# Two transformer blocks in float32 on one core: how the last expert pairs are combined and written

## The chip, the core and the metric

One core of a Trainium2 chip runs the whole program. The metric is the device time of one execution in microseconds, as the median of several runs. The engines are named as in the profile: PE (TensorE, matrix products), DVE (VectorE), ACT (ScalarE), POOL (GpSimd), SP (SyncE, which here only issues transfers). Everything is float32, so that a product of 128 x 128 with 128 x 512 is two MATMUL records on PE.

## The reference, cut to what matters

There are two blocks over 512 tokens of width 1024. The first has an SSD mixer, attention and a feed-forward part; the second has attention, an mLSTM branch and, at its end, a mixture of 32 experts. Only this end matters here:

```python
h = rmsnorm_2(x, norm2_g)
# each token: one group of 8 experts, in it the two best, weights top_w
y_row = (silu(xb @ w_gate[e]) * (xb @ w_up[e])) @ w_down[e]      # 1024 -> 512 -> 1024
y = zeros((T, D)).at[row_tok].add(y_row * row_w)                 # two rows per token
out = x + y
```

## The kernel before, in words

The 512 tokens are four tiles of 128 (`xtok[:, t, :]`, in SBUF, tokens on partitions). Each expert has room for 64 rows, and the experts are taken in 16 pairs, so that a pair fills 128 rows. Experts 0 and 1 are pair 0, and so on to pair 15, the last one.

For a pair, PE (function `pair` in the tensor block) multiplies the rows of the pair, which it picked out of `xtok` with a 0/1 matrix in `pick_rows`, with the gate slabs of its two experts, then with the up slabs (L1436, `both_k`: two products side by side in the two halves of the array), picks the rows of the next pair (L1445), transposes the inner rows `hE` (L1452, `turn_inner`) and multiplies with the down slabs (L1436 again) into banks 6 and 7. ACT applies Silu (L2849), copies the transposed inner rows (L2854) and empties banks 6 and 7 into `ysb` (L2858, L2861). For pairs 0 to 14 ACT then writes `ysb` to the scratch tensor `ys_d` in HBM (L2864). DVE multiplies gate and up (L2437), scales the picked rows (L2429) and makes the 0/1 matrices `pick` for the pair after the next (`picks`, L2400 and L2404). With `weighted=True` it makes another one, `wpick` (L2409, L2413), in which a token's router weight stands instead of the 1.

A slab is a [128 x 4096] tile, 2 MB. There are nine places for slabs (`ws`), used in turn (`turn9`). SP issues all slab loads in one order in its queue (`next_slab`, L607): two gate slabs, two up slabs, two down slabs of each pair, each as soon as the product that used its place has ended (`g_full`, `uu_full`, `yy_full` count these products).

The last pair does not go through `ys_d`. PE transposes `wpick` (L1469), ACT copies it to `wpT` (L2852), and PE multiplies it with `ysb` into the eight banks (L1531, eight products of 128 x 128 with 128 x 512, in the order `LAST`). All other rows are fetched by POOL: after the last write to `ys_d` (`y_st`) it gathers, for each tile and each of the token's two experts, 128 rows of 4 KB (L2938, eight gathers of 512 KB into the places `ws[7]` and `ws[8]`; rows that belong to the last pair read zeros, which POOL wrote at the start, L2923). DVE adds each gather times its weight to `xtok` (L2497), and after all of these the eight banks (L2503). `comb` counts those sums, and SP writes tile after tile to `out` (L617). The order on each engine is the order of the code.

## Time and profile before

| | before |
|---|---|
| median of 3 runs | 1761.68 us (1761.37 to 1761.73) |
| profiled execution | 1762.02 us |
| its span, first to last instruction | 1760.2 us |
| PE busy | 1701.0 us, 97% |
| DVE busy | 775.6 us, 44% |
| ACT busy | 329.4 us, 19% |
| POOL busy | 18.7 us, 1% |
| HBM read, written | 319.66 MB, 18.37 MB |
| mean granted clock of PE | 0.987 |

PE is called busy nearly throughout, but a busy share says little of what bounds a stage, since records of products overlap and their ends are modelled. For the last stage one reads what the DMA engines do in a stretch, then the chain of waits from the end backwards, then each engine by time.

### The profile page before, as it was taken

The numbers are of one execution on the slowest core, as the hardware profiler recorded it, in microseconds if no ns is written. First come the engines' busy times: TensorE is split into PE (matmuls) and PEld (weight loads), VectorE is DVE, ScalarE is ACT, GpSimd is POOL, SyncE is SP. The second block draws the span as 40 slices with busy tenths as digits, with TensorE's granted clock in tenths as the row PEclk, the third lists the DMA queues.
The fourth block names the chain that finished last, engine by engine and source line by source line (L and its number), as shares of the span: only waits on it lengthen the run. The fifth ranks groups of instructions, "written<-read, shape, count | busy, mean of one in ns | idle before, by whom it ended". The sixth has DMA issues, their size and how long they took to land.

```text
span 1760.2 us, 19911 instructions
## 1 busy us (share of the span) xinstructions
PE 1701.0 (97%) x7884; PEld 1054.2 (60%) x7884; DVE 775.6 (44%) x1711; ACT 329.4 (19%) x691; POOL 18.7 (1%) x39
## 2 busy tenths in 40 slices
PE   8999999999999999999999999999799999999997
PEld 5445544488888888878444454447645455544452
DVE  4322448677777772354796233325522121211123
ACT  1121224231111100120234234201200000000000
POOL 0001000000000000000000000000000000000001
PEclk9999999999999999999999999999899999999999
DMA  9874120022122213141211110313489999999997
GB/s 404 330 281 161 60 95 2 1 81 96 57 86 95 81 67 131 48 158 54 96 48 49 48 48 1 143 48 143 189 349 428 429 429 429 429 429 429 429 428 316
DMA packets 30248, 335.62 MB, mean 191 GB/s; under 512 B 3208, under 2 KB 5784, under 8 KB 10592
## 3 DMA queue, kind: packets, MB, share of 16 engines
q1 hardware_dynamic: 22464, 310.56, 43.4%
q10 hardware_dynamic: 5168, 14.91, 2.2%
q0 software_dynamic: 2544, 9.18, 1.5%
q8 instruction: 47, 0.77, 0.2%
q14 instruction: 25, 0.20, 0.0%
HBM read 319.66 MB, written 18.37 MB: 192 GB/s over the span
## 4 chain that ended last, share of the span: by engine, by line
PE 85%; DMA 6%; DVE 6%; ACT 2%; issue 1%; POOL 0%; SPq 0%; DVEq 0%; ACTq 0%; POOLq 0%
PE bank L1436 15%; PE bank L1039 15%; PE bank L1087 8%; PE bank L1445 6%; PE bank L1222 5%; PE bank L646 4%; PE bank L850 3%; PE bank L1230 3%; PE bank L1131 3%; PE bank L1394 3%; PE bank L1180 3%; DMA arena<-in_w_expert_up 2%; DMA pool<-in_w_expert_up 2%; PE bank L995 2%; PE bank L628 2%; PE bank L840 2%
## 5 line engine op out<-in xcount | busy, mean ns | idle before, releaser
L1436 PE MATMUL bank<-pool,arena 128*64 128x512 f32 x1216 | 337.8, 598 | 8.5 <-DMA pool<-in_w_expert_up 3.9
L1039 PE MATMUL bank<-pool 128*128 128x256 f32 x1232 | 267.6, 381 | 0.8 <-ACT pool L2510 0.8
L1039 PEld LDWEIGHTS bank<-pool 128*128 128x128 f32 x1232 | 235.5, 191 | 32.8 <-issue 1.0
L1436 PEld LDWEIGHTS bank<-pool,arena 128*64 128x64 f32 x1216 | 108.0, 138 | 175.9 <-issue 167.6
L2437 DVE TENSOR_TENSOR arena<-arena,bank 128x512 f32<-128x512 f32 x16 | 11.0, 688 | 281.5 <-PE bank L1436 281.5
L1445 PE MATMUL bank<-arena 128*128 128x128 f32 x1024 | 123.7, 281 | 8.5 <-DVE arena L2404 8.5
L1445 PEld LDWEIGHTS bank<-arena 128*128 128x128 f32 x1024 | 119.4, 196 | 20.8 <-issue 12.2
L1222 PE MATMUL bank<-pool 128*128 128x512 f32 x256 | 114.5, 595 | 1.9 <-DVE arena L2203 1.9
L1222 PEld LDWEIGHTS bank<-pool 128*128 128x128 f32 x256 | 47.4, 190 | 58.4 <-issue 54.9
L1436 PE MATMUL bank<-xT,arena 128*64 128x512 f32 x160 | 72.3, 606 | 3.8 <-DMA pool<-in_w_expert_up 3.8
L1436 PE MATMUL bank<-arena 128*64 128x512 f32 x160 | 70.3, 593 | 0.0
L2429 DVE TENSOR_TENSOR arena<-bank,cols 128x512 f32<-128x512 f32 x32 | 22.1, 692 | 103.6 <-PE bank L1445 103.6
L646 PE MATMUL bank<-pool 128*128 128x512 f32 x144 | 63.8, 597 | 0.0
L1180 PE MATMUL bank<-pool 128*128 128x512 f32 x128 | 60.7, 610 | 1.5 <-ACT arena L2510 1.5
L2694 ACT ACTIVATE arena<-arena,cols 128x512 f32<-128x512 f32 x44 | 29.4, 714 | 173.1 <-DVE arena L1940 173.1
L1087 PE MATMUL bank<-arena,pool 128*128 128x256 f32 x264 | 58.5, 379 | 0.0
L850 PE MATMUL bank<-pool 128*128 128x512 f32 x128 | 56.7, 594 | 0.0
L1087 PEld LDWEIGHTS bank<-arena,pool 128*128 128x128 f32 x264 | 50.3, 190 | 6.7
L2510 ACT ACT_TABLE_LOAD x39 | 50.0, 1283 | 19.5 <-DVE small L1649 16.9
L1847 DVE TENSOR_TENSOR pool<-pool 128x1024 f32<-128x1024 f32 x44 | 52.8, 1220 | 0.3
L2510 ACT ACTIVATE arena<-bank 128x512 f32<-128x512 f32 (+4 forms) x62 | 29.2, 490 | 119.4 <-PE bank L646 51.3
L2510 ACT ACTIVATE pool<-bank 128x512 f32<-128x512 f32 (+3 forms) x73 | 31.4, 462 | 96.0 <-PE bank L850 45.2
(418 smaller groups left out, 2180.8 us busy)
## 6 DMA issues: line engine op xcount, KB each, us to landing
pool<-in_w_expert_gate SPq DMA_DIRECT2D x27, 2048.0 KB, 25.8
pool<-in_w_expert_down SPq DMA_DIRECT2D x27, 2048.0 KB, 28.0
pool<-in_w_expert_up SPq DMA_DIRECT2D x22, 2048.0 KB, 23.2
pool<-in_w_in SPq DMA_DIRECT2D x15, 2048.0 KB, 8.2
pool<-in_w_ada SPq DMA_DIRECT2D x12, 2048.0 KB, 19.2
pool<-in_w_up SPq DMA_DIRECT2D x11, 2048.0 KB, 8.0
arena<-in_w_expert_gate SPq DMA_DIRECT2D x5, 2048.0 KB, 29.8
xT<-in_w_expert_up SPq DMA_DIRECT2D x5, 2048.0 KB, 24.8
```

The source lines that it names most:

```text
L646: ins = pe.matmul(bank[home[g]][:, :], w[:, k, c0:c0 + P], src[:, k, :], start=(k == 0), stop=(k == KD - 1))
L850: ins = pe.matmul(bank[home[g0 + c]][:, :], w[:, k, c * P:(c + 1) * P], hT[:, k, :], start=(k == 0), stop=(k == KD - 1))
L1039: ins = pe.matmul(up_quarter(u, p), lhs[:, k, :], rhs[:, k, :], start=(k == 0), stop=(k == 3))
L1087: ins = pe.matmul(dst, lhs[:, i, :], rhs[:, i, :], start=(i == 0 and p in (0, 1, 4)), stop=(i == HP - 1), skip_group_check=p not in (0, 1, 4))
L1131: ins = pe.matmul(bank[qa_bank(u, p)][:, 0:256], lhs[:, k, :], rhs[:, k, :], start=(k == 0 and p in (0, 1, 4)), stop=(k == 3), skip_group_ ...
L1180: ins = pe.matmul(bank[home[g0 + t]][:, :], hT[:, k, t * P:(t + 1) * P], w[:, k, :], start=(k == 0), stop=(k == KD - 1))
L1222: ins = pe.matmul(bank[home[g]][:, :], w[:, k, o:o + P], hT[:, k, :], start=(k == 0), stop=(k == KD - 1))
L1230: ins = pe.matmul(bank[home[g]][:, :], w[:, k, m * P:(m + 1) * P], src[:, k, :], start=(k == 0), stop=(k == 3))
L1394: ins = pe.matmul(dst, lhs[:, k, :], rhs[:, k, :], start=(k == 0 and p in (0, 1, 4)), stop=(k == 3), skip_group_check=p not in (0, 1, 4))
L1436: ins = pe.matmul(dst[b * CAP:(b + 1) * CAP, :], lhs(b, k), rhs(b, k), start=(k == 0), stop=(k == n_k - 1))
L1445: ins = pe.matmul(bank[x][:, f * P:f * P + n], xtok[:, t, c], pick[:, t, 0:n], start=(t == 0), stop=(t == NT - 1))
L2510: ins = nc.scalar.activation(dst, src, f, **kw)
```

## The change

The rows of pair 14 are no longer written to `ys_d` and gathered. DVE makes a weighted matrix for it too (`wpick2`), PE transposes it in pair 14 (`weights_turned`), and multiplies it with `ysb` in the last pair's body: two products behind the gate product, three behind the up product, three behind the transposes of the inner rows (`combined`), into banks 0 and 1 in turn; DVE adds each to `xtok` (`summed`). The gathers of tiles 0 and 1 start when pair 13's rows are written and pair 14's up product has ended; they go to `ws[6]`, and DVE adds them before it multiplies gate and up of the last pair. The gathers of tiles 2 and 3 go to `ws[7]` and wait until the last down slabs have landed. The two last down slabs are loaded in halves of their columns (first halves of both, then second halves), the down product of the last pair signals each half, ACT empties each half, `LAST` goes over the four tiles by column halves, and the sums and writes to `out` are by halves too. One more block of zeros is written to `ys_d` at the start. Three semaphores that guarded what other waits guard as well are gone (`alog_exp`, `z_sig`, `ov_sp`).

```diff
-        LAST = ((0, 0), (1, 0), (0, 1), (1, 1), (2, 0), (2, 1), (3, 0), (3, 1))
+        LAST = tuple((t, half) for half in range(2) for t in range(4))
@@ SP
-                for r in range(15):
+                for r in range(13):
                     next_slab(4, r)
-                for t in range(NT):
-                    sp.wait_ge(S["comb"], LAST.index((t, 1)) + 1)
-                    sp.dma_start(out[t * P:(t + 1) * P, :], xtok[:, t, :]).then_inc(S["out_st"], 16)
+                sp.wait_ge(S["g_full"], 15)
+                sp.wait_ge(S["uu_full"], 15)
+                for half in range(2):
+                    c = slice(half * 512, (half + 1) * 512)
+                    for b in range(2):
+                        at = turn9[(6 * 15 + 4 + b) % 9]
+                        sp.dma_start(slot(at, 4, D)[:, :, c], down_of(30 + b).rearrange("p (k n) -> p k n", n=D)[:, :, c])\
+                          .then_inc(S["ed_half"] if half else landed[at], 16)
+                for n, (t, half) in enumerate(LAST):
+                    c = slice(half * 512, (half + 1) * 512)
+                    sp.wait_ge(S["comb"], 9 + n)
+                    sp.dma_start(out[t * P:(t + 1) * P, c], xtok[:, t, c]).then_inc(S["out_st"], 16)
@@ PE
+                def weights_turned(n):
+                    pe.wait_ge(S["pick_rdy"], E // 2 + 2 * n)
+                    if n:
+                        pe.wait_ge(S["wp_ev"], 1)
+                    for t in range(NT):
+                        ins = pe.transpose(bank[5][:, t * P:(t + 1) * P], (wpick2, wpick)[n][:, t, :], ident[:, :])
+                    ins.then_inc(S["wp_full"], 1)
+                def combined(n0, n1):
+                    pe.wait_ge(S["wp_ev"], 1)
+                    pe.wait_ge(S["yy_ev"], E // 2 - 1)
+                    for n in range(n0, n1):
+                        t, half = LAST[n]
+                        if n >= 2:
+                            pe.wait_ge(S["comb"], n - 1)
+                        pe.matmul(bank[n % 2][:, :], wpT2[:, t, :], ysb[:, half * 512:(half + 1) * 512], start=True, stop=True)\
+                          .then_inc(S["add_full"], 1)
@@ PE, pair(p, at, first, last, late)
+                        if last and half == 0:
+                            combined(0, 2)
...
+                        weights_turned(1)
+                        combined(2, 5)
                     pe.wait_ge(S["he_rdy"], p + 1)
                     turn_inner()
...
+                    else:
+                        combined(5, 8)
+                    if late:
+                        weights_turned(0)
...
+                        if last and half:
+                            pe.wait_ge(S["ed_half"], 32)
@@ DVE
+                pair(E // 2 - 4, False, False)
+                picks(E // 2 - 2, weighted=wpick2)
                 pair(E // 2 - 3, False, False)
-                picks(E // 2 - 1, weighted=True)
+                picks(E // 2 - 1, weighted=wpick, more=1)
                 pair(E // 2 - 2, False, False)
-                pair(E // 2 - 1, False, True)
+                gathered(0)
+                summed(0, 2, lambda n: n % 2)
+                gathered(1)
+                pair(E // 2 - 1, False, True)
+                summed(2, 8, lambda n: n % 2)
+                summed(8, 10, lambda n: n % 8)
+                gathered(2)
+                summed(10, 11, lambda n: n % 8)
+                gathered(3)
+                summed(11, 16, lambda n: n % 8)
@@ POOL
-            for r0 in range((E - 2) * CAP, ROWS, P):
+            for r0 in range(ZR, ROWS, P):
...
-                po.wait_ge(S["y_st"], 16 * (E // 2 - 1))
+                po.wait_ge(S["y_st"], 16 * (E // 2 - 2))
+                po.wait_ge(S["uu_full"], E // 2 - 1)
                 for t in range(NT):
+                    if t == 2:
+                        po.wait_ge(S["yy_full"], E // 2 - 1)
+                        po.wait_ge(S["ed_half"], 32)
```

`gathered(t)` waits for its gathers (one semaphore for tiles 0 and 1, another for 2 and 3) and makes the two weighted additions of the tile; `summed(n0, n1, ...)` adds the banks of those combining products, each to half a tile.

## Rows read from the trace of the kernel before

**Rows 1.** Windows by stage: engines' busy time, granted clock, DMA share, GB/s.

```profile
core 0: us, PE busy (x) PEld busy (x) DVE busy (x) ACT busy (x) POOL busy (x), PEclk, DMA share, GB/s
1400.00:1450.00 50.00, 50.00 (x298) 26.54 (x296) 9.80 (x26) 3.16 (x6) 0.00 (x0) 1.00 1.01 429
1720.00:1730.00 10.00, 7.82 (x38) 2.79 (x36) 0.00 (x0) 0.60 (x1) 0.65 (x1) 1.00 1.01 428
1740.00:1750.00 10.00, 9.22 (x32) 3.68 (x29) 8.99 (x7) 1.08 (x2) 0.00 (x0) 0.96 0.46 184
```

**Rows 2.** Chain of waits, last 60 us: start us, us, what.

```profile
1705.45 0.44 PE bank L1452 x4
...
1717.93 10.57 DMA ys_d<-arena
...
1733.21 7.53 DMA xT<-ys_d,smi
...
1740.76 1.29 DVE arena L2497
...
1751.33 1.88 DVE arena L2503 x3
```

**Rows 3.** Timeline of PE: start us, us, line, what, idle time before it.

```profile
1664.37 0.61 PE L1436 MATMUL bank<-xT,arena 128*64 128x512 f32 x1 [2.00 <-DMA pool<-in_w_expert_up]
...
1721.46 1.89 PE L1436 MATMUL bank<-pool,arena 128*64 128x512 f32 x8
1725.53 7.09 PE L1436 MATMUL bank<-pool,arena 128*64 128x512 f32 x32 [2.18 <-DMA pool<-in_w_expert_up]
...
1736.19 8.78 PE L1436 MATMUL bank<-pool,arena 128*64 128x512 f32 x32 [2.07 <-DMA pool<-in_w_expert_down]
1745.75 7.10 PE L1531 MATMUL bank<-arena 128*128 128x512 f32 x16 [0.78 <-ACT arena L2858]
```

**Rows 4.** Window over the zero fill, and POOL's wait behind it.

```profile
150.00:185.00 35.00, 35.00 (x143) 19.28 (x142) 13.10 (x30) 7.22 (x12) 7.36 (x10) 1.00 0.55 173
...
POOL arena L2926 <- PE bank L1087: 591.0, 1, 591.0
```

**Rows 5.** Timeline of DVE, pairs 13 to 15 and the end.

```profile
1673.25 0.69 DVE L2437 TENSOR_TENSOR arena<-arena,bank 128x512 f32<-128x512 f32 x1 [21.17 <-PE bank L1436]
...
1684.48 2.14 DVE L2409 TENSOR_SCALAR arena<-arena,small 128x128 f32<-128x128 f32 x8
1686.66 0.69 DVE L2413 TENSOR_TENSOR arena<-arena 128x512 f32<-128x512 f32 x1
1701.79 0.69 DVE L2437 TENSOR_TENSOR arena<-arena,bank 128x512 f32<-128x512 f32 x1 [14.44 <-PE bank L1436]
...
1750.01 1.28 DVE L2497 SCALAR_TENSOR_TENSOR arena<-xT,small,arena 128x1024 f32<-128x1024 f32 x1
1751.33 4.87 DVE L2503 TENSOR_TENSOR arena<-arena,bank 128x512 f32<-128x512 f32 x8
```

**Rows 6.** DMA queues in 1721:1728, 1729:1735, 1753:1760.2: packets, MB, share.

```profile
q1 hardware_dynamic: 164, 2.42, 80.9%
q10 hardware_dynamic: 143, 0.52, 18.3%
...
q1 hardware_dynamic: 150, 2.13, 83.3%
q0 software_dynamic: 90, 0.35, 14.5%
...
GB/s 0 0 0 0 0 0 478 410 364 387 410 432 387 387 455 432 387 364 410 364 364 478 364 455 455 387 410 364 364 478 364 455 432 387 228 0 0 0 0 0
q1 hardware_dynamic: 576, 2.10, 73.0%
```

**Rows 7.** Timeline: issues of ACT and SP.

```profile
1689.40 0.34 ACTq L2864 DMA_DIRECT2D ys_d<-arena  x1
...
1695.23 6.82 SPq L607 DMA_DIRECT2D pool<-in_w_expert_down  x2
...
1701.73 0.33 SPq L607 DMA_DIRECT2D pool<-in_w_expert_down  x1
...
1753.23 3.32 SPq L617 DMA_DIRECT2D out<-arena  x4
```

**Rows 8.** Windows of 3 us behind three of PE's waits; columns as in rows 1.

```profile
1666.00:1669.00 3.00, 3.00 (x8) 0.91 (x6) 0.00 (x0) 0.00 (x0) 0.00 (x0) 0.50 0.99 421
...
1726.00:1729.00 3.00, 3.00 (x17) 1.20 (x15) 0.00 (x0) 0.00 (x0) 0.00 (x0) 1.00 1.04 445
...
1738.00:1741.00 3.00, 3.00 (x10) 0.98 (x8) 0.24 (x1) 0.00 (x0) 0.93 (x1) 0.53 1.03 410
```

More of the change, by code:

```diff
@@ L396, in two_blocks @@
                             ("i15", (OVB + 1,)),
-                            ("la", (NT, 36)), ("g7", (7,)), ("cm", (E, 7)), ("pre", (NT, E)), ("bs", (E,)), ("row", (P,)), ("slo", (2, NT))):
+                            ("la", (NT, 36)), ("g7", (7,)), ("cm", (E, 7)), ("pre", (NT, E)), ("bs", (E,)), ("row", (P,)), ("slo", (2, NT)))
+        for name, shape in RS:
             R[name] = view(arena, r_at, *shape)
@@ L401, in two_blocks @@
         wt = sm(2, NT)
+        wpick2 = R["be"].rearrange("p a b -> p (a b)").rearrange("p (t s) -> p t s", s=P)
+        at_ = [n for n, _ in RS].index("oh1")
+        wpT2 = view(arena, 13312 + sum(int(np.prod(w)) for _, w in RS[:at_]), NT, P)
         io_i = smi[:, 0:32]
@@ L1453, in turn_inner, with pair @@
                     ins.then_inc(S["ht_full"], 1)
-                def pair(p, at, first=False, last=False):
+                def weights_turned(n):
[14 more added lines that the diff above has]
+                          .then_inc(S["add_full"], 1)
+                def pair(p, at, first=False, last=False, late=False):
                     pe.wait_ge(S["xt_ev"], p * 2 + 2)
@@ L1525, in _ @@
                 for p in range(13, E // 2):
-                    pair(p, [placed(0, 6 * p + c) for c in range(6)], last=(p == E // 2 - 1))
-                pe.wait_ge(S["xt_ev"], E + 1)
+                    pair(p, [placed(0, 6 * p + c) for c in range(6)], last=(p == E // 2 - 1), late=(p == E // 2 - 2))
+                pe.wait_ge(S["wp_ev"], 2)
+                pe.wait_ge(S["comb"], 8)
                 for n, (t, half) in enumerate(LAST):
@@ L2393, in _, with picks @@
                 seq(ve.tensor_copy(slot_i, R["sl"].rearrange("p b t -> p (b t)")))
-                def picks(i, weighted=False):
+                def picks(i, weighted=None, more=0):
                     for t in range(NT):
@@ L2402, in picks @@
                     ins.then_inc(S["pick_part"], 1)
-                    ve.wait_ge(S["pick_part"], i * 2 + 1)
+                    ve.wait_ge(S["pick_part"], i * 2 + (more + 1))
                     ve.tensor_tensor(pick, pick, pickb, ALU.add).then_inc(S["pick_rdy"], 1)
-                    if weighted:
-                        ve.wait_ge(S["pick_rdy"], i + 1)
+                    if weighted is not None:
+                        ve.wait_ge(S["pick_rdy"], i + more + 1)
                         for t in range(NT):
-                            for b, dst_ in enumerate((wpick, pickb)):
+                            for b, dst_ in enumerate((weighted, pickb)):
                                 ins = ve.tensor_scalar(dst_[:, t, :], R["row"], R["sl"][:, b, t:t + 1], wt[:, b, t:t + 1],
@@ L2612, in _ @@
                 ac.wait_ge(S["ld_rows"], 16)
-                act(expa, row("a_log"), ACT.Exp, "alog_exp")
+                act(expa, row("a_log"), ACT.Exp)
                 ac.wait_ge(S["lx_rdy"], 1)
@@ L2785, in _ @@
                 own("act_free")
-                act(omtok, omtok, ACT.Sigmoid, "z_sig")
+                act(omtok, omtok, ACT.Sigmoid)
                 for x in range(2 * MH):
@@ L2844, in _, with pair @@
             if on("end"):
-                def pair(p, first, last):
+                def pair(p, first, last, late=False):
                     ac.wait_ge(S["g_full"], p + 1)
@@ L2850, in pair @@
                     if last:
-                        ac.wait_ge(S["xt_full"], E + 1)
-                        nc.scalar.activation(wpT.rearrange("p t s -> p (t s)"), bank[5][:, :], ACT.Copy).then_inc(S["xt_ev"], 1)
+                        ac.wait_ge(S["wp_full"], 2)
+                        nc.scalar.activation(wpT.rearrange("p t s -> p (t s)"), bank[5][:, :], ACT.Copy).then_inc(S["wp_ev"], 1)
                     ac.wait_ge(S["ht_full"], p + 1)
                     nc.scalar.activation(hET.rearrange("p k r -> p (k r)"), bank[4][:, :], ACT.Copy).then_inc(S["ht_ev"], 1)
+                    if late:
+                        ac.wait_ge(S["wp_full"], 1)
+                        nc.scalar.activation(wpT2.rearrange("p t s -> p (t s)"), bank[5][:, :], ACT.Copy).then_inc(S["wp_ev"], 1)
                     ac.wait_ge(S["yy_full"], p + 1)
-                    if not first:
+                    if last:
+                        ac.wait_ge(S["add_full"], 8)
+                    elif not first:
                         ac.wait_ge(S["y_st"], p * 16)
@@ L2860, in pair @@
                         ins.then_inc(S["yy_ev"], 1)
+                        ac.wait_ge(S["yy_full"], p + 2)
                     nc.scalar.activation(ysb[:, 512:D], bank[7][:, :], ACT.Copy).then_inc(S["yy_ev"], 1)
-                    if not last:
+                    if not last and not late:
                         ac.wait_ge(S["yy_ev"], p + 1)
@@ L2888, in _ @@
                 pair(0, True, False)
-                with ac.Fori(1, E // 2 - 1) as p:
+                with ac.Fori(1, E // 2 - 2) as p:
                     pair(p, False, False)
+                pair(E // 2 - 2, False, False, late=True)
                 pair(E // 2 - 1, False, True)
```

65 lines of the change are left out of this document (33 added, 32 removed).

## The prediction

> **What bounds the kernel now.** I read first the windows by stage: from 1300 us to about 1744 us the DMA engines are full, at 428 to 429 GB/s while PE is "busy" beside them [rows 1]. This is the stream of expert slabs (2.1 MB each, 4.9 us at that rate), six of them for each of 16 pairs of experts. Then the chain of waits, from its end backwards [rows 2]: sums of DVE from the matmul banks (L2503), eight weighted additions of gathered rows (L2497), the wait for the gathers, their issues by POOL, the write of pair 14's rows to `ys_d`, and before that PE. The chain ends in DVE: gathered rows of tile 0 are there at 1740.76, then 8 additions of 1.32 us and 8 sums of 0.61 us, 15.4 us without a hole, then the last writes. Third, PE by time [rows 3]: it waits 2.18 us for the last up slab (starts 1725.53), 2.07 us for the last down slab (starts 1736.19), ends the down product at 1744.97 and the eight combining products at 1752.85, 3.4 us before DVE. So PE has slack behind the last slabs, DVE has none, and the last slabs are early enough. The question is what the change does to these three.
>
> **Removed waits and bookkeeping.** `alog_exp`, `z_sig`, `ov_sp` and the tenth block of zero fill (instead of nine) are all before or outside the last stage. The fill lies at 161 to 178 us, with DMA share 0.55 [rows 4], and POOL, its issuer, then waits 591 us for other work; another 512 KB there is covered. If its cover were gone it would cost 1.3 us. The removed waits stand behind waits on the same or a later event; taken at 0, bound plus or minus 0.1. `picks(14)` now also makes weights: 8 tensor_scalar and one addition, 2.14 + 0.69 us of DVE [rows 5], in a pair in which DVE idles over 20 us: 0.
>
> **The write of pair 14 goes.** 0.52 MB leave the stream [rows 6]; that is 1.2 us of DMA, of which some 0.2 MB (0.5 us) had gone ahead of the last up slab. POOL need not wait for it: its gathers now hang on pair 13's write (issued 1689.40; the next one took 10.57 us to land [rows 2, 7]) and on pair 14's up product, whose end released SP at 1701.73 and DVE at 1701.79 [rows 5, 7].
>
> **Gathers of tiles 0 and 1, early.** Four of the eight go from behind the last slabs to before them. POOL is released at about 1701.8 instead of 1728.5. In the trace a gather's bytes begin to flow some 4.5 us after the release under the full stream: q0 has moved 0.35 MB by 1735 [rows 6]. So 1706.5 here. How fast do they go against the stream? The nearest row is the write to `ys_d`, 0.52 MB in pieces of 4 KB like the gather's: it takes about 6 us and the slabs get 2.42 MB in the 7 us around it [rows 6]. Four gathers take so some 24 us, to about 1730.5. Their 2.1 MB are paid by the slabs, since the engines were full. Ahead of the last up slab pass 1.9 MB, 4.4 us at 429 GB/s; less the 0.5 us of the write that went: the last up slab lands 3.8 us later (bounds: 2.5, if the gathers share worse; 4.4, if all of them pass). **PE starts its up product at 1729.3 instead of 1725.53.** This is the term that decides.
> Here the Trainium skill says another thing: "DMA: Bandwidth & Descriptors", Queues, rings and completion order, has each DMA engine change between queues only after a whole packet of typically 9 to 17 descriptors. A write of 8 pieces per engine would by that be through in little over a microsecond; in this trace it takes 6 us, so the trace does not agree. By the page all four gathers would be ahead of the last up slab, and the sum would be 0.6 us more.
>
> **Down slabs by halves.** Both are issued at 1701.7; before, one was issued at 1695.23 and the other at 1701.73. With at least three slabs still queued nothing runs dry. The pieces are 2 KB instead of 16 KB. The trace shows 4 KB pieces at about 400 GB/s (the writes to `out` [rows 6]), slabs at 429; I take 390, and half of the rate as the other bound. First halves land near 1734, second ones near 1740 (1748 at half rate). PE asks for them at 1744.0 and 1747.5 (below), so this costs 0; at half rate it just touches.
>
> **PE behind the up slab.** Two of the eight combining products for pair 14's rows lie in PE's wait for the slab (0.89 us each, 7.10 us for eight [rows 3]), and so do the transposes of pair 14's weights (0.44 us, like those of L1452 [rows 2]): free. PE ended its gate product at 1723.35; with these 2.2 us it is 1725.6, and the wait is still 3.7 us. Behind a wait of 2.00 us and one of 2.07 us PE's granted clock fell to 1.2 GHz (0.50 and 0.53 of full in slices of 3 us), and the down product took 8.78 instead of 7.04 us; behind one of 2.18 us it stayed at 2.4 GHz [rows 2, 3, 8]. I expect a fall here, and 1.4 us for it (0 to 1.74: part of it may lie in the idle time). Then, one after the other: up product 7.09, transposes of weights 0.44, three products 2.66, transposes of the inner rows 0.44, three products 2.66, down product 7.04 at full clock. Together 20.33 + 1.4 = 21.7, so **PE ends its down product at 1751.0**, against 1744.97.
>
> **DVE beside it.** Before `hE` of the last pair DVE now has, in its order, two tiles of gathered rows and two sums: 2.64 + 1.22 + 2.64 = 6.5 us from the landing of gather 4. Landing near 1731 makes it free at 1737.5, up product done at 1737.8: covered by 0.3 us only. PE's fifth product waits for the third sum, likewise within 0.5 us. Taken at 0, bound +1.7.
>
> **Gathers of tiles 2 and 3** wait for the second halves: 1740 + 4.5 us for the four issues and the start + 3.5 to 5 us of data gives 1748 to 1749. POOL queues nothing behind them. DVE asks for them at 1753.5: covered by over 4 us.
>
> **The end.** Behind 1751.0: two products (1.78) and a sum (0.69) for the sums that DVE does before it takes gathered rows, to 1753.5. Then tile 2 (2.64), one sum (0.61), tile 3 (2.64), five sums (3.05): 8.94, to 1762.4. PE's other products (done 1758.1) are not late. Last write: 0.85 us from issue to first bytes as at 1753.23, 0.65 us for 256 KB, 0.9 from the last bytes to the end, as in the rows [rows 6, 7], with 0.1 of queue: 2.5. **End 1764.9 against 1760.2: +4.7 us.** The profiled execution is 1762.02, 0.34 over the median, so the median becomes 1761.68 + 4.7 = 1766.4 (+0.27%).
> The same page of the Trainium skill, Bandwidth, says to batch DMAs to 1 MiB or more, and gives 2.0 us plus the bytes at 436 GB/s for one. That speaks against writes of 256 KB. Here four writes of 512 KB went back to back, 2.10 MB in about 5.3 us [rows 6], so a fixed part does not add up and I leave it out; by the page, with the last six writes one behind the other, the end would be near 1772.
>
> **Rivals.**
> 1. *The clock stays at 2.4 GHz and the gathers share worse.* 1.4 and 1.3 us less: +2.0, 1763.7. For it: one wait of 2.18 us had no fall. Against: the wait is longer now.
> 2. *The early gathers cost the stream nothing.* If the slabs kept their time and lost only the write, the up product would start at 1725.0, the down product end at 1745.3 (its clock is not cut by a 3.6 us wait), and 13.9 us behind it the span ends at 1759.2: -1.0 us, 1760.7. It decides while the up product starts not later than 1726.0. DMA at 428 GB/s throughout speaks against it. More gain is not to be had: DVE needs 11.4 us behind the down product however early the gathers are.
> 3. *DVE is held by gathers 0 to 3.* If they land after 1731.3, every further microsecond goes to `hE`, the transposes and the down product. Landing at 1734 makes +7.2, 1768.9.
> 4. *The change does not do what it says*: the second gathers or half slabs late by over 5 us, for instance at half rate with a late start; +8 or more.
> 5. *The writes by halves each pay in full.* The six that follow 1757 at 2.4 us each (0.85 + 0.65 + 0.9, from the rows) end at 1771.4, which makes 1772.9. Against: four writes went back to back. The Trainium skill's rule above would make it so.
>
> **How the numbers follow.** About 0.2%, 3.5 us, is what a measurement can tell here. Forecast as worked out 0.50 (1765.2 to 1768.0), rival 1 0.20, rival 2 0.11, rival 3 0.10, rival 4 0.02, rival 5 0.01, none of these 0.06. Slower: 0.50 + 0.10 + 0.02 + 0.01, less 0.03 of the forecast that may fall below 1765.2: 0.60. Same: 0.20 + 0.11 + 0.03 = 0.34. Faster: 0.06, what no case here covers. Range: from the upper edge of rival 2, 1761.2, to rival 3's middle, 1769.2.
>
> **What would show it.** PE's wait for the last up slab at 3 to 4 us and its start near 1729; the granted clock under 1 in the slices behind it; gather 4 landed near 1731; down product ended near 1751; DVE from 1753.5 without a hole. Wrong is it if the up product starts before 1727, if DVE has holes behind the down product (then gathers bind), or if `hE` begins over 1 us after the up product ends.

## The result, and the profile after

| | before | changed |
|---|---|---|
| median of 11 runs | 1761.37 us (1759.39 to 1762.03) | 1766.18 us (1765.10 to 1767.56) |
| ratio of the medians' runs | | 1.003, 95% interval 1.0023 to 1.0038 |
| profiled execution, its span | 1762.02, 1760.2 us | 1765.10, 1763.3 us |

The changed kernel is slower by 4.8 us, 0.27%, where 4.7 us were forecast. The interval of the ratio leaves out 1, so the loss is clear, though small. The two profiled executions lie only 3.1 us apart: that of before was nearly the slowest of its runs, that of the changed kernel the fastest. So first come the same stretches of both, then a way to line them up.

The windows of the changed kernel that answer to rows 1 (columns as there). The engines for transfers are as full as before up to 1730 us, but from 1720 us on they move 404 instead of 428 GB/s, and 387 GB/s from 1730 to 1735 us, where the slabs' pieces are of 2 KB. Behind 1740 us only gathers are left.

```profile
1400.00:1450.00 50.00, 50.00 (x298) 26.63 (x296) 9.81 (x26) 3.96 (x7) 0.00 (x0) 1.00 1.01 429
1720.00:1730.00 10.00, 9.00 (x38) 3.10 (x36) 1.28 (x1) 0.60 (x1) 0.00 (x0) 1.00 1.01 404
1740.00:1750.00 10.00, 10.00 (x40) 3.38 (x40) 2.08 (x4) 1.20 (x2) 3.28 (x4) 1.00 0.61 210
```

PE by time in the changed kernel (answers to rows 3). L1450 is `both_k`, L1486 the combining products for pair 14, L1475 and L1466 the transposes, L1573 the last eight products.

```profile
1693.28 0.74 PE L1450 MATMUL bank<-pool,arena 128*64 128x512 f32 x1 [2.24 <-DMA arena<-in_w_expert_up]
...
1693.81 1.06 PE L1450 MATMUL bank<-pool,arena 128*64 128x512 f32 x1
...
1724.09 1.98 PE L1486 MATMUL bank<-arena 128*128 128x512 f32 x4
1727.08 7.09 PE L1450 MATMUL bank<-pool,arena 128*64 128x512 f32 x32 [1.00 <-DMA pool<-in_w_expert_up]
1734.10 0.65 PE L1475 MATMUL bank<-ident,arena 128*128 128x128 f32 x4
1734.59 1.88 PE L1486 MATMUL bank<-arena 128*128 128x512 f32 x4
1736.89 1.12 PE L1486 MATMUL bank<-arena 128*128 128x512 f32 x2 [0.42 <-DVE arena L2553]
1737.86 0.60 PE L1466 MATMUL bank<-ident,arena 128*128 128x128 f32 x4
1738.29 2.93 PE L1486 MATMUL bank<-arena 128*128 128x512 f32 x6
1741.15 7.09 PE L1450 MATMUL bank<-pool,arena 128*64 128x512 f32 x32
1748.17 7.13 PE L1573 MATMUL bank<-arena 128*128 128x512 f32 x16
```

PE starts the last up product at 1727.08 instead of 1725.53. Between its end and the down product it now has six products, and it ends the down product at 1748.2 (7.09 us from 1741.15), before at 1744.97.

DVE by time in the changed kernel (answers to rows 5); L2543 are gathered rows, L2553 sums, L2479 is `hE`:

```profile
1728.69 2.60 DVE L2543 SCALAR_TENSOR_TENSOR arena<-arena,small 128x1024 f32<-128x1024 f32 x2 [18.12 <-DMA arena<-ys_d,smi]
1731.33 1.48 DVE L2553 TENSOR_TENSOR arena<-arena,bank 128x512 f32<-128x512 f32 x2
1732.91 2.60 DVE L2543 SCALAR_TENSOR_TENSOR arena<-arena,small 128x1024 f32<-128x1024 f32 x2
1735.55 0.69 DVE L2479 TENSOR_TENSOR arena<-arena,bank 128x512 f32<-128x512 f32 x1
...
1749.33 0.69 DVE L2553 TENSOR_TENSOR arena<-arena,bank 128x512 f32<-128x512 f32 x1 [7.39 <-PE bank L1573]
1750.19 0.69 DVE L2553 TENSOR_TENSOR arena<-arena,bank 128x512 f32<-128x512 f32 x1 [0.17 <-PE bank L1573]
1750.98 2.60 DVE L2543 SCALAR_TENSOR_TENSOR arena<-pool,small,arena 128x1024 f32<-128x1024 f32 x2
1753.62 0.69 DVE L2553 TENSOR_TENSOR arena<-arena,bank 128x512 f32<-128x512 f32 x1
1754.41 2.60 DVE L2543 SCALAR_TENSOR_TENSOR arena<-pool,small,arena 128x1024 f32<-128x1024 f32 x2
1757.05 3.85 DVE L2553 TENSOR_TENSOR arena<-arena,bank 128x512 f32<-128x512 f32 x5
```

The early gathers are there at 1728.69, but DVE's own order (tile 0, two sums, tile 1) ends at 1735.5, 1.4 us behind the up product (about 1734.15), and only then comes `hE`. Ahead of its first sum behind the down product DVE idles 7.4 us; from there on it has no hole but one of 0.17 us. Its work ends at 1760.9 and the span 2.4 us later.

The chain that ended last says which of these set the time (it answers to rows 2):

```profile
1706.82 21.84 DMA arena<-ys_d,smi
...
1728.69 1.30 DVE arena L2543
...
1735.55 0.04 DVE arena L2479
...
1736.89 1.12 PE bank L1486 x2
...
1741.22 7.02 PE bank L1450 x32
1748.24 5.36 PE bank L1573 x12
```

It does not run through PE's wait for the last up slab. It runs through the early gathers, DVE's work ahead of `hE`, and a combining product that waits for DVE's third sum. PE's own path lies close behind (e3 shows by how much).

**Lining the executions up.** All kernels here are the same up to pair 14's second down slab. The transfer records of each trace give the time of that slab's first bytes (each whole slab is 128 records of 16 KB, which can be counted back from the last one); I call it the mark (1698.39 before, 1696.55 changed). The whole stage is full of transfers, so what lies ahead of the mark does not depend on the change. From the mark to the end it is 61.8 us before and 66.8 us changed: 5.0 us more, which agrees with the medians. By the same records the last up slab is complete 25.7 us behind the mark before and 29.7 us changed, 4.0 us later. The table is read in that way: "up at" is the start of the last up product behind the mark, "rest" from there to the end of the span, "fall" the product during which the granted clock fell (14: pair 14's up product, 15: the last pair's).

| kernel | PE's wait for the last up slab | up at | rest | together | fall | median, us |
|---|---|---|---|---|---|---|
| before | 2.18 | 27.1 | 34.6 | 61.8 | last down | 1761.37 |
| before again (e12b) | 2.25 | 27.2 | 34.6 | 61.9 | 15 | 1761.69 |
| changed | 1.00 | 30.5 | 36.3 | 66.8 | 14 | 1766.18 |
| e1 | 4.59 | 31.6 | 35.2 | 66.8 | 14, 15 | 1765.64 |
| e2 | 0 | 29.7 | 37.5 | 67.2 | 14 | 1765.93 |
| e3 | 0.97 | 30.5 | 35.8 | 66.3 | 14 | 1765.42 |
| e4 | 0.99 | 30.4 | 35.8 | 66.2 | 14 | 1765.51 |
| e5 | 3.28 | 30.7 | 33.7 | 64.4 | none | 1764.10 |
| e6 | 3.35 | 31.0 | 38.5 | 69.5 | 15 | 1770.80 |
| e7 | 0.98 | 30.5 | 38.5 | 68.9 | 14 | 1768.55 |
| e8 | 3.33 | 30.8 | 32.7 | 63.5 | 15 | 1761.85 |
| e9 | 0 | 29.4 | 31.1 | 60.5 | 14 | 1759.00 |
| e10 | 0 | 27.2 | 33.4 | 60.6 | none | 1759.24 |
| e11b | 0 | 29.5 | 31.2 | 60.6 | 14 | 1759.01 |

Medians of the experiments come from 5 to 12 runs, spread over 2 to 6 us, so that differences under about 1 us between two of them are told by the traces alone, which are one execution each. The ratios are to the kernel before as it ran beside each experiment (medians 1761.13 to 1761.36 us).

### The profile page after: what moved, and what is told of

Same layout as the page of the kernel before. It is cut to its first block, busy times and chain, and to the rows that moved or that the text cites. A ratio compares the mean times of both kernels' runs of the same rounds, so it can differ in the third digit from the quotient of the medians.

```text
span 1763.3 us, 19985 instructions
## 1 busy us (share of the span) xinstructions
PE 1707.2 (97%) x7904; PEld 1054.6 (60%) x7904; DVE 784.3 (44%) x1728; ACT 330.2 (19%) x692; POOL 19.5 (1%) x40
## 4 chain that ended last, share of the span: by engine, by line
PE 83%; DMA 8%; DVE 6%; ACT 2%; issue 1%; POOL 0%; SPq 0%; DVEq 0%; ACTq 0%; POOLq 0%
PE bank L1053 15%; PE bank L1450 14%; PE bank L1101 8%; PE bank L1459 5%; PE bank L1236 5%; PE bank L660 4%; DMA pool<-in_w_expert_up 4%; PE bank L864 3%; PE bank L1244 3%; PE bank L1145 3%; PE bank L1408 3%; PE bank L1194 3%; DMA arena<-in_w_expert_up 2%; PE bank L1009 2%; PE bank L642 2%; PE bank L854 2%
## 5 line engine op out<-in xcount | busy, mean ns | idle before, releaser
L1450 PE MATMUL bank<-pool,arena 128*64 128x512 f32 x1216 | 337.8, 598 | 7.7 <-DMA arena<-in_w_expert_up 3.9
L1053 PEld LDWEIGHTS bank<-pool 128*128 128x128 f32 x1232 | 234.5, 190 | 32.6 <-issue 0.7
L1450 PEld LDWEIGHTS bank<-pool,arena 128*64 128x64 f32 x1216 | 107.4, 138 | 177.2 <-issue 168.5
L2479 DVE TENSOR_TENSOR arena<-arena,bank 128x512 f32<-128x512 f32 x16 | 11.0, 687 | 258.6 <-PE bank L1450 258.6
L1236 PEld LDWEIGHTS bank<-pool 128*128 128x128 f32 x256 | 47.4, 190 | 58.4 <-issue 55.0
L1450 PE MATMUL bank<-xT,arena 128*64 128x512 f32 x160 | 70.6, 594 | 2.1 <-DMA pool<-in_w_expert_up 2.1
L1450 PE MATMUL bank<-arena 128*64 128x512 f32 x160 | 72.1, 604 | 0.0
L2755 ACT ACTIVATE arena<-arena,cols 128x512 f32<-128x512 f32 x44 | 29.4, 714 | 171.7 <-DVE arena L1981 171.7
```

Of the source, the lines that this page charges most:

```text
L1053: ins = pe.matmul(up_quarter(u, p), lhs[:, k, :], rhs[:, k, :], start=(k == 0), stop=(k == 3))
L1236: ins = pe.matmul(bank[home[g]][:, :], w[:, k, o:o + P], hT[:, k, :], start=(k == 0), stop=(k == KD - 1))
L1450: ins = pe.matmul(dst[b * CAP:(b + 1) * CAP, :], lhs(b, k), rhs(b, k), start=(k == 0), stop=(k == n_k - 1))
```

## The experiments

**e1: the load alone, in the kernel before.**

```diff
...
+                po.wait_ge(S["y_st"], 16 * (E // 2 - 2))
+                po.wait_ge(S["uu_full"], E // 2 - 1)
+                for t in range(4):
+                    po.dma_start(ws[6][:, t * D:(t + 1) * D], a["w_expert_up_2"][t * P:(t + 1) * P, 0:D]).then_inc(S["ov_sp"], 16)
                 po.wait_ge(S["y_st"], 16 * (E // 2 - 1))
...
```

> The kernel before, with four transfers of 512 KB in pieces of 4 KB added on POOL's queue (slab rows into ws[6], nobody reads them) at the time and in the place where the change has its early gathers. Theory A (the early gathers' bytes push the last slabs): the last up product starts about 3.5 us later against the stream, the last down slab lands 4.9 us later, end +4 to +5 us over the kernel before. Rival B (the stream has room, the loss comes from the products that the change puts between up and down product): end within +1 us of the kernel before.

Measured: ratio 1.0026 (1.0017 to 1.0035), 1765.64 us, +4.5 on the kernel before. PE by time in e1:

```profile
1728.04 8.63 PE L1435 MATMUL bank<-pool,arena 128*64 128x512 f32 x32 [4.59 <-DMA pool<-in_w_expert_up]
...
1739.89 7.09 PE L1435 MATMUL bank<-pool,arena 128*64 128x512 f32 x32 [1.73 <-issue]
```

PE waits 4.59 us for its last up slab instead of 2.2, and starts 4.4 us later behind the mark. Nothing of PE's or DVE's work was changed. So 2.1 MB put ahead of the last slabs cost 4.5 us by themselves: theory A stands, rival B falls for this kernel. But here they do not cost it through PE. The chain of e1 runs through the write to `ys_d` and the gathers, as in the kernel before: DVE starts its eight additions 47.4 us behind the mark instead of 42.4 and has no hole from there on. e1 shows that early bytes push back all that comes behind them, not which of the things pushed back ends the changed kernel.

The queues of the changed kernel between 1708 and 1722 us show how they share (packets, MB, share):

```profile
q1 hardware_dynamic: 320, 4.72, 79.4%
q0 software_dynamic: 320, 1.18, 21.0%
```

For each piece of 16 KB of the slabs one piece of 4 KB of the gathers goes, 320 against 320: the bytes are 4 to 1. The first gather's 128 pieces, eight for each of the 16 engines, take from 1707.1 to 1713.3 us, 6.2 us. That is the pace that was taken from the write to `ys_d` in rows 6, and it speaks again against the rule of the Trainium skill in "DMA: Bandwidth & Descriptors", Queues, rings and completion order, by which whole packets of 9 to 17 descriptors would alternate and a gather would be through in about one turn of each engine.

**e2: all gathers behind the last slabs.** The changed kernel, with

```diff
                 po.wait_ge(S["uu_full"], E // 2 - 1)
+                po.wait_ge(S["ed_half"], 32)
@@ DVE: tiles 0 and 1 behind the eighth sum
-                gathered(0)
                 summed(0, 2, lambda n: n % 2)
-                gathered(1)
                 pair(E // 2 - 1, False, True)
                 summed(2, 8, lambda n: n % 2)
+                gathered(0)
+                gathered(1)
```

> The changed kernel with all eight gathers behind the last slabs (POOL waits for the second halves before the first gather too), and DVE takes tiles 0 and 1 behind the third to eighth sum. Theory A: PE's last up product starts 3 to 4 us earlier against the stream than in the changed kernel, and the down product ends 4 to 5 us earlier; but DVE then waits for gathers, so the end is +3 to +5 us over the kernel before, no gain on the changed kernel. Rival B: the down product ends within 1 us of where it ends in the changed kernel.

Measured: 1.0027 (1.0018 to 1.0036), 1765.93 us. The end is as expected, but the steps that were to make it are not. The down product ends 1.3 us earlier behind the mark than in the changed kernel, which is neither theory A's 4 to 5 us nor within rival B's 1 us. The up product starts only 0.8 us earlier behind the mark than in the changed kernel (29.7, not 27), and without any wait for its slab. In this execution PE itself was late. In pair 14 it had waited 2.25 us for an up slab and the clock had fallen (as in the changed kernel's profile, first two lines of PE's rows above: 1.06 us a product instead of 0.59), which cost 1.7 us as such falls do elsewhere (8.78 against 7.09 us for a product), and the transposes and two products of the change cost 2.4 us more. The wait that was to cover them had been used up. So where the fall comes in pair 14, PE's added work and the gathers' bytes are two bounds within 1 us of each other.

**e3: order of DVE ahead of `hE`.** Of e2's edit only the DVE part.

> The changed kernel, but DVE takes gathered tiles 0 and 1 behind the third to eighth sum instead of ahead of hE. Theory A: hE starts 1.4 us earlier against the end of the up product, down product ends 0.8 to 1.4 us earlier, the median is 0.8 to 1.4 us below the changed kernel. Rival C (DVE's place before hE is covered by PE's other work): 0.

Measured: 1.0021 (1.0012 to 1.003), 1765.42 us. In the trace `hE` starts with the end of the up product, and from the start of the up product to the end of the down product it is 20.7 us instead of 21.2. The median is 0.8 us lower, at the lower end of what was expected, and no clear difference; the trace gives 0.5. `hE` starts 1.3 us earlier against the up product, as theory A says, but only 0.5 us of it reach the down product. The hold is real and small: PE's own path, from the up slab through the six products, is 0.5 us shorter than the one through the gathers and DVE.

**e4: pace of the sums.** Each sum waits in the code for DVE's own sum before it (`own("comb")`). e4 makes that wait once per group.

```diff
+                    own("comb")
                     for n in range(n0, n1):
                         ...
                         ve.wait_ge(S["add_full"], n + 1)
-                        own("comb")
```

> The changed kernel, but a sum waits for DVE's own last sum only once per group of sums instead of each time. Theory D: sums go from 0.79 back to 0.61 us apiece and the tail of six sums loses 1.1 us, the median falls by 0.8 to 1.1 us. Rival E: the writes by halves (about 0.8 us apart in the trace) are then the pace, and the gain is 0.4 us or less.

Measured: 1.0025 (1.0015 to 1.0034), 1765.51 us. The last five sums take 3.08 us instead of 3.85 (0.62 apiece, not 0.77), but the span then ends 2.8 us behind DVE instead of 2.4: of 0.8 us gained on DVE 0.4 reach the end. By this trace rival E holds, the writes are nearly the pace; the median, 0.7 us lower, lies between the two.

**e5: without the six products between up and down product.**

```diff
-                        combined(2, 5)
...
-                    else:
-                        combined(5, 8)
...
-                summed(2, 8, lambda n: n % 2)
...
```

The waits that counted these sums are lowered to match. Most of pair 14's rows are thus missing in the output.

> The changed kernel without the six combining products for pair 14 that lie between the up product and the down product of the last pair, and without their six sums (so pair 14's rows are missing in most of the output). Theory A, as it stands after the first four experiments (the path is up product, six products, down product, then DVE): the down product ends about 5 us earlier. Rival F (the gathers of tiles 2 and 3 are the next bound right behind it, they are ready about 1 us before DVE asks in the changed kernel): the end gains 1.5 us or less. Without F the end gains 5 us too.

Measured: 1.0017 (1.0008 to 1.0026), 1764.10 us, 2.1 us below the changed kernel. DVE by time in e5, behind the down product (which ends at 1745.4, 47.9 behind the mark, against 51.7):

```profile
1747.42 0.69 DVE L2550 TENSOR_TENSOR arena<-arena,bank 128x512 f32<-128x512 f32 x1 [0.17 <-PE bank L1570]
1749.63 2.61 DVE L2540 SCALAR_TENSOR_TENSOR arena<-pool,small,arena 128x1024 f32<-128x1024 f32 x2 [1.51 <-DMA pool<-ys_d,smi]
```

The down product gains 3.8 us, not 5, and the end 2.1 us by the median, 2.4 by the trace. DVE now waits 1.51 us for the gathers of tiles 2 and 3. They are the next bound, as rival F says, though the gain is somewhat over its 1.5.

**e6: the last down slabs whole.**

```diff
-                for half in range(2):
-                    c = slice(half * 512, (half + 1) * 512)
-                    for b in range(2):
-                        at = turn9[(6 * 15 + 4 + b) % 9]
-                        sp.dma_start(slot(at, 4, D)[:, :, c], down_of(30 + b)...[:, :, c])...
+                for b in range(2):
+                    at = turn9[(6 * 15 + 4 + b) % 9]
+                    sp.dma_start(ws[at][:, :], down_of(30 + b)).then_inc(landed[at], 16)
...
```

> The changed kernel with the last two down slabs loaded whole again; PE and POOL wait for whole slabs. PE asks for the first half of the down product at 1741.2 and the first halves are there by 1733; whole slabs would be there near 1738. All theories: 0 within 0.7 us. If it is slower by over 1.5 us, the halves matter. If it is faster by 0.5 to 1 us, the 2 KB pieces cost stream time ahead of the second gathers.

Measured: 1.0054 (1.004 to 1.0068), 1770.80 us: 4.6 us slower than the changed kernel, where all theories said 0. PE does not wait for the down slabs in either. DVE by time in e6:

```profile
1732.04 2.60 DVE L2538 SCALAR_TENSOR_TENSOR arena<-arena,small 128x1024 f32<-128x1024 f32 x2 [23.06 <-DMA arena<-ys_d,smi]
...
1738.90 0.69 DVE L2474 TENSOR_TENSOR arena<-arena,bank 128x512 f32<-128x512 f32 x1
```

and the queues from 1724.3 to 1728 us, first in the changed kernel, then in e6:

```profile
q1 hardware_dynamic: 311, 0.79, 55.2%
q0 software_dynamic: 183, 0.62, 42.6%
```

```profile
q1 hardware_dynamic: 89, 1.20, 76.3%
q0 software_dynamic: 89, 0.36, 23.9%
```

Since the queues take turns by pieces, a gather gets a fifth of the stream beside pieces of 16 KB and nearly half beside a mixture with pieces of 2 KB. The halves let the early gathers get through: they are ready 3.3 us earlier on the clock, 2.7 us against the mark. Without them `hE` starts 1.9 us behind the up product (8.78 us from 1728.18, with the clock fall), and DVE holds PE: rival 3 of the prediction, by a cause that it did not name. From DVE's first addition of early rows to the end of the down product it is 19.55 us in both kernels (1728.69 to 1748.24, 1732.04 to 1751.59), and from there to the end 15.1 us. So the trace's 2.7 us come by the gathers alone, and the clock fall in e6's up product is hidden behind them. The trace has 2.7 us of the 4.6; the rest of the median's difference is open (five runs, 1768.66 to 1772.61; the profile is of the fastest).

**e7: writes of whole tiles.**

```diff
-                for n, (t, half) in enumerate(LAST):
-                    c = slice(half * 512, (half + 1) * 512)
-                    sp.wait_ge(S["comb"], 9 + n)
-                    sp.dma_start(out[t * P:(t + 1) * P, c], xtok[:, t, c]).then_inc(S["out_st"], 16)
+                for t in range(NT):
+                    sp.wait_ge(S["comb"], 9 + LAST.index((t, 1)))
+                    sp.dma_start(out[t * P:(t + 1) * P, :], xtok[:, t, :]).then_inc(S["out_st"], 16)
```

> The changed kernel with four writes of whole tiles instead of eight of halves; sums stay by halves, so a tile is ready only with its second half. Theory: the last four writes of 1.3 us each start with the sum of (0, 1), near 1758.5, and end at 1763.8 + 0.9: +1.0 to +1.5 us over the changed kernel. Rival (a fixed cost per write counts more than its bytes): 0 or a gain.

Measured: 1.0041 (1.0027 to 1.0055), 1768.55 us, 2.4 us over the changed kernel; the trace gives 2.1. The four writes are issued from 1758.47 on and DVE ends at 1760.8, but the span at 1765.4: 4.6 us behind DVE instead of 2.4. The direction is the theory's, the size was set too low by 1 us. The writes by halves are a gain by themselves. It is a smaller one against the kernel before, which summed tile by tile: there the span ended 4.0 us behind DVE.

**e8: all gathered rows before the last sums.** The changed kernel with e4's edit and the following (`slab_landed(c)` waits until slab number c has landed; the last down slabs are 94 and 95)

```diff
-                gathered(0)
                 summed(0, 2, lambda n: n % 2)
+                gathered(0)
                 gathered(1)
                 pair(E // 2 - 1, False, True)
                 summed(2, 8, lambda n: n % 2)
-                summed(8, 10, lambda n: n % 8)
                 gathered(2)
-                summed(10, 11, lambda n: n % 8)
                 gathered(3)
-                summed(11, 16, lambda n: n % 8)
+                summed(8, 16, lambda n: n % 8)
@@ POOL, tiles 2 and 3
-                        po.wait_ge(S["ed_half"], 32)
+                        slab_landed(94)      # first halves of the last two down slabs
+                        slab_landed(95)
```

> The changed kernel with three edits: DVE makes the two first sums before tiles 0 and 1, the gathers of tiles 2 and 3 wait only for the first halves of the last down slabs, and DVE takes them all before the last eight sums, which wait for DVE's own work once. Theory A: hE is not held up (down product 0.7 to 1.4 us earlier); gathers of tiles 2 and 3 are there near 1745, both tiles are added by 1750.5, and the last eight sums follow PE's products, so that the end lies 10.3 us behind the down product instead of 15: the median is 4 to 6 us below the changed kernel, that is 0 to 1.5 us below the kernel before. Rival G (the gathers, contending with the second halves, make the down product wait): the down product ends 1 to 3 us later, gain on the changed kernel 2 us or less.

Measured: 1.0002 (0.9993 to 1.0011), 1761.85 us: 4.3 us below the changed kernel, level with the kernel before. From the end of the down product (1750.9) to the end it is 10.2 us. The down product does not end earlier, as was expected, but 1.5 us later (53.2 behind the mark against 51.7), since the clock fell in the up product of this execution. Rival G falls, PE does not wait for the second halves. The early gathers still go ahead of the up slab here, and the kernel is 4.3 us faster all the same. What each of the three edits gives of it was not measured, beyond e4's part.

**e9: only tile 0 early.** e8 with tile 1's gathers behind `slab_landed(92)` (the first up slab of pair 15), and DVE taking tile 0, two sums, tile 1.

> The kernel of e8 with only tile 0 gathered early; tile 1's gathers wait for pair 15's first up slab, so that nearly none of their bytes go ahead of the second one. DVE: tile 0, two sums, tile 1, hE. Theory A (bytes ahead of the last up slab cost PE time while PE waits for it): the up product starts 1.0 to 1.8 us earlier against the stream than in e8 where PE waits for the slab, PE's wait is 1 to 2 us instead of 3.3, and the median falls by 1 to 2.5 us against e8, to 1759.5 to 1761. Rival H (tile 1 lands too late and DVE holds hE): hE starts over 1 us after the up product ends and the median is at or over e8's.

**e10: no gather ahead of that up slab.** e8 with `slab_landed(92)` ahead of all gathers, and tiles 0 to 3 together between the eighth and the ninth sum.

> The kernel of e8 with all four gathers of tiles 0 and 1 released by the landing of pair 15's first up slab, and DVE taking all four tiles between the eighth and the ninth sum. Theory A: the up product starts as early as in the kernel before plus at most 1 us, the down product ends 2 to 4 us before e8's, but DVE has four tiles (10.5 us) behind the eighth sum and then eight sums, so that DVE ends the kernel: median 1760.5 to 1762.5. Rival I (DVE's tail is not the bound): 3 us below e8.

Measured: e9 0.9989 (0.998 to 0.9998), 1759.00 us; e10 0.999 (0.9981 to 0.9999), 1759.24 us. Both are faster than the kernel before by about 2 us by the medians and 1.2 to 1.4 us by the traces, a gain at the limit of what these runs can tell. The median of e9 is 2.9 us below e8's, somewhat more than expected. Its up product starts 1.4 us earlier than e8's, as expected, but without any wait, since the clock fell in pair 14; `hE` starts 0.2 us behind it, so rival H falls. The median of e10 is 2.6 us below e8's, under theory A's range and near rival I's 3. PE by time in e10:

```profile
1722.96 7.09 PE L1450 MATMUL bank<-pool,arena 128*64 128x512 f32 x32
...
1736.61 7.09 PE L1450 MATMUL bank<-pool,arena 128*64 128x512 f32 x32
1743.63 7.13 PE L1573 MATMUL bank<-arena 128*128 128x512 f32 x16
```

and DVE:

```profile
1737.52 5.25 DVE L2543 SCALAR_TENSOR_TENSOR arena<-arena,small 128x1024 f32<-128x1024 f32 x4
1743.09 5.25 DVE L2543 SCALAR_TENSOR_TENSOR arena<-pool,small,arena 128x1024 f32<-128x1024 f32 x4 [0.33 <-DMA pool<-ys_d,smi]
1748.37 4.87 DVE L2553 TENSOR_TENSOR arena<-arena,bank 128x512 f32<-128x512 f32 x8
```

With the bytes behind the last up slab, that slab is complete 25.8 us behind the mark and the up product starts at 27.2, as in the kernel before, against 30.7 to 31.0 in the three executions with early gathers in which the clock did not fall in pair 14 (e5, e6, e8): 3.6 us is the price of the early gathers where PE has to wait for the slab. The down product ends 5.3 us earlier behind the mark than in e8, 1.7 of which are the clock fall; 2 to 4 were expected. DVE then is the bound, as expected: from 1737.5 on it works with one hole of 0.33 us, for the gathers of tiles 2 and 3, although the products are ready from 1744.5 on.

**e11b: tile 0 ahead of `hE`.** e10 with its own semaphore for tile 0, `gathered(0)` behind the two first sums, the other tiles as in e10.

> The kernel of e10 (all gathers from the landing of pair 15's first up slab on), but DVE adds tile 0 as soon as it is there, between the two first sums and hE, and the other three tiles behind the eighth sum. Theory: DVE was the bound in e10 (it ends its four tiles at 1748.3, with PE's products ready from 1744.5 on), so 2.6 us leave its tail; tile 0 is there about 4.7 us behind the start of the up product, so that hE waits at most 0.5 us. Median 1.0 to 2.5 us below e10, 1757 to 1758.5. Rival (tile 0 lands later and holds hE): equal to e10 or above it.

Measured: 0.999 (0.9981 to 0.9999), 1759.01 us, no gain on e10 that can be told. `hE` is not held up, and DVE is done with all tiles at 1748.96, but in this execution the clock fell in pair 14 and PE came to the up product at 29.5 behind the mark; its last product then ends the kernel (the last sum waits 0.17 us for PE). That is not all that kept the 1 to 2.5 us away. DVE, now earlier, waits 0.79 us for the gathers of tiles 2 and 3, and is done with all tiles 52.7 us behind the mark, against 52.6 in e10. DVE starts on these two tiles 47.3 to 47.4 us behind the mark in e9, e10 and e11b alike, and waits for their gathers in all three. So without the fall too the gain could not have been over about 0.4 us; the theory had left these gathers out. The three kernels end 60.5 to 60.6 us behind the mark, where PE's path and the one through the second gathers are nearly of one length.

**e12b: the kernel before, again.**

> The kernel before, unchanged, once more, for a second profile of it: its median should be within 0.5 us of its other runs. In it I look whether the last up product again waits for its slab, by how much, and whether the clock falls stand at other places than in the first profile; both kernels' last stages can then be compared in two executions each.

Measured: 1761.69 us, ratio 1.0006 (0.9997 to 1.0015). PE by time:

```profile
1724.13 8.78 PE L1436 MATMUL bank<-pool,arena 128*64 128x512 f32 x32 [2.25 <-DMA pool<-in_w_expert_up]
...
1735.30 7.09 PE L1436 MATMUL bank<-pool,arena 128*64 128x512 f32 x32 [0.89 <-ACT arena L2854]
```

The wait for the slab is the same, but the clock fell in the up product and not in the down product. From the mark it is 61.9 us to the end, 61.8 in the first profile: between these two places the fall is of no account in this kernel, since DVE and the gathers end it.

## Why the prediction was right, and which of its steps were not

The sum had four terms. With the mark they can be read one by one (before to changed, us):

| term | forecast | measured |
|---|---|---|
| start of the last up product | +3.8 | +3.4 (27.1 to 30.5) |
| from there to the end of the down product | 19.4 to 21.7 | 19.4 to 21.2 |
| from there to the end of DVE's work | 11.2 to 11.4 | 11.2 to 12.7 |
| from there to the end | 4.0 to 2.5 | 4.0 to 2.4 |
| together | +4.7 | +5.0 |

- *Early gathers delay the last up slab: right.* The slab is complete 4.0 us later, where 3.8 was forecast (4.4 less 0.5 is 3.9, a slip of 0.1). e1 shows it alone (+4.4 for PE's start there, where nothing was taken from the stream in return), e10 shows it gone. The pace was read from the right row. The gathers were ready 32.1 us behind the mark; 1731, which is 32.6, was forecast. That it fits so well is in part luck: their bytes began 10.6 us behind the mark and not 8.1, since the up product of pair 14 that releases them ended 2.2 us later by the clock fall, and the last gather took 3.2 us instead of 6, beside pieces of 2 KB.
- *Two products and the transposes are free in PE's wait: right, with little to spare.* PE still waits about 1.0 us for the slab where the clock fell in pair 14 and 3.3 us where it did not. With fewer bytes ahead of the slab (e2, e9, e11b, all with the fall in pair 14) no wait is left, and PE's own work sets the start at 29.4 to 29.7, 0.8 to 1.2 us before the changed kernel's. The forecast had no account of where the clock falls ahead of the last pair.
- *A wait of 3.7 us and 1.4 us for the clock: the step that failed in the profiled execution*, with a wait of 1.00 us and no fall. It came in others: waits of 3.3 us in e5, e6 and e8, with a fall in two of the three.
- *DVE ahead of `hE` covered by 0.3 us, bound 1.7: missed, inside its bound.* DVE held `hE` by 1.4 us. The prediction had named "over 1 us" as a sign of being wrong, and on the path it was: the chain that ended last runs through the early gathers and DVE, not through PE's wait for the up slab. From the up product's start to the down product's end it is 0.8 us more than the sum of its parts at full clock (21.16 against 20.33), of which e3 gives back 0.5. The gathers were in time; the up product, without the fall, was done earlier than forecast, and DVE's work took 6.9 us, not 6.5.
- *Eleven microseconds of DVE behind the down product: too low by 1.3.* The sums were put at 0.61 us from rows 5, where they wait for nothing of DVE's own. The change has each wait for the last one (0.77 to 0.79 us). That wait stands in the code and was not costed. e4 shows it, and that half of it is hidden behind the writes.
- *Second gathers covered by over 4 us: too rosy.* Their last bytes come at 1749.2 and DVE asks at 1750.98. e5 shows them as the next bound.
- *Half slabs cost nothing: right for PE, which never waits for them, but not the whole of it.* Their small pieces are what let the last early gather through (e6: 2.7 us by the trace, 4.6 by the median). The forecast took every gather beside pieces of 16 KB.
- *Writes by halves: right.* They were counted at 1.5 us of gain on the kernel before, and 4.0 to 2.4 is 1.6. Rival 5, writes that each pay in full, falls: it had the end at 1771.4, and it came at 1763.3.
- *Rivals 2 and 3:* rival 2's start at 1725.0 did not go with the prediction's own 1725.6 for PE, and rival 3's landing at 1734 makes +7.4 and not +7.2. Neither touches the forecast.

So the clock term (1.4 too much) and the start of the up product (0.4 too much) stood against `hE` (0.8) and the sums (1.3 too little). The direction and its first cause, the early bytes, were understood. That the total was hit within 0.3 us is luck.

What the loss comes from has two answers that do not add up to one sum. The 2.1 MB ahead of the slab that PE needs next cost 3.6 us of PE's start where PE has to wait for it, and moving them behind it gains 2.6 us by the medians (e8 to e10). The order of DVE's work, the wait within each sum and an unneeded wait of POOL cost 4.3 us: e8 puts these right with the early bytes still in place, and is level with before. e9 to e11b do both and are about 2 us faster than the kernel before (upper ends of the intervals at 0.9998 and 0.9999).

## What to carry to other kernels

In a stage in which transfers run at their limit, an earlier transfer is not free: ask which transfer it goes ahead of, and who waits for that one. Release it by the landing of the last thing that is needed before it, not by the place in SBUF becoming free. And before work is moved into an engine's wait, look whether that wait is there in each execution or is sometimes eaten by a slower clock.

## What the runs showed of the hardware that was not expected

Two queues that both have work share the transfer engines piece by piece, here for pieces of 2, 4 and 16 KB. Beside 16 KB pieces the gathers' 4 KB pieces got a fifth (1.18 MB against 4.72 in 14 us, 320 records each). Beside the 2 KB pieces of the half slabs they got two thirds (e10, 1723 to 1730 us):

```profile
q0 software_dynamic: 495, 1.83, 66.6%
q1 hardware_dynamic: 491, 0.98, 36.7%
```

The layout of a transfer so decides how fast another one goes: with the slabs in halves the same four gathers were ready 2.7 us earlier against the mark.

Gathers that are released on idle queues were slower than ones queued before. Queues of the changed kernel, 1740 to 1750 us, with no other transfer:

```profile
DMA packets 576, 2.10 MB, mean 210 GB/s; under 512 B 64, under 2 KB 64, under 8 KB 576
```

Their bytes take from 1741.2 to 1749.2 us by the transfer records, 8 us for 2.1 MB, while before 3.23 MB of gathers passed between 1736 and 1744. The four gathers begin 1.7 to 2.0 us apart, but POOL issues them 1.24 us apart, so its pace alone does not explain it. The cause is open.

The granted clock fell to 1.2 GHz behind waits of PE of 1.96 to 4.59 us in most cases of these profiles and not behind others of 2.18 and 3.28 us, and the same kernel (before, e12b) had the fall in the down product in one execution and in the up product in the other. Each fall cost 1.5 to 1.75 us of the product it hit.
